# Two transformer blocks on one core: weights stored in load order, and the second attention by pairs of heads

## What is computed

```python
# block 1: attention, short convolution, then a mixture of experts
for g in range(N_GROUPS):                     # 4 groups of 8 experts, D_EXPERT = 256
    act = silu(einsum('nd,edf->nef', h, w_gate[sl])) * einsum('nd,edf->nef', h, w_up[sl])
    act = act * combine[:, g, :, None]        # 2 experts of 32 for each token
    y = y + einsum('nef,efd->nd', act, w_down[sl])
# block 2: grouped attention with 8 heads of 64 on 2 key heads, 512 + 256 keys
s = einsum('bqkgd,btkd->bkgqt', qblk, k) * scale
p = softmax(s.astype(float32), axis=-1)
o = einsum('bkgqt,btkd->bqkgd', p, v)
# beside it a long convolution, gates, and at the end a layer of
# 16384 small experts with 16 picks for each of 8 heads of a token
```

## Time and profile before

| | |
|---|---|
| median of 3 runs | 2894.65 us (2886.13 to 2894.65) |
| the profiled execution's own time | 2893.39 us |
| its span | 2891.6 us |
| mean granted PE clock, share of full | 0.957 |
| busy: PE, DVE, ACT, POOL | 2607.6, 1564.7, 1055.6, 516.1 us |
| DMA | 294127 packets, 605.99 MB |

### The profile page before, as it was taken

The page is one execution under the profiler, slowest core; times in us unless marked ns, Lnnn a source line. Parts: engine busy times, 40 slices in busy tenths (PEclk is TensorE's granted clock), DMA queues, the critical chain, the costliest instruction groups (busy, mean ns, idle before and its releaser), DMA issues.

```text
span 2891.6 us, 31507 instructions
## 1 busy us (share of the span) xinstructions
PE 2607.6 (90%) x12520; PEld 1910.5 (66%) x12520; DVE 1564.7 (54%) x2920; ACT 1055.6 (37%) x1317; POOL 516.1 (18%) x427
## 2 busy tenths in 40 slices
PE   6998997667778899999989999988888999999997
PEld 4666685422234344655768999988888877777775
DVE  4533244321126656454542998899998444444444
ACT  5754432120004311565233333444554333333332
POOL 0100000000010000000000011133334255555550
PEclk9999998788887999999999999999999999999998
DMA  5543442899980000201122466778999898989992
GB/s 184 196 146 117 174 146 89 279 375 371 376 323 30 29 29 29 88 30 40 48 89 88 157 228 230 257 265 319 349 350 345 292 315 312 323 312 323 312 325 90
DMA packets 294127, 605.99 MB, mean 210 GB/s; under 512 B 16503, under 2 KB 157943, under 8 KB 283800
## 3 DMA queue, kind: packets, MB, share of 16 engines
q1 hardware_dynamic: 223072, 384.33, 38.5%
q0 software_dynamic: 44528, 154.69, 14.9%
q10 hardware_dynamic: 26376, 64.90, 5.9%
HBM read 533.08 MB, written 70.78 MB: 209 GB/s over the span
## 4 chain that ended last, share of the span: by engine, by line
PE 62%; DVE 17%; DMA 8%; ACT 5%; SPq 4%; issue 3%; ACTq 0%; DVEq 0%
PE P L2670 6%; PE P L2671 6%; PE P L2672 6%; DVE window L592 4%; SPq L2759 4%; DMA ug<-in_ur,sparse 4%; PE P L2550 3%; PE P L2551 3%; PE P L2552 3%; PE P L2390 3%; DVE part L592 2%; PE P L2215 2%; PE P L2621 2%; PE P L2018 2%; DVE ug L1381 2%
## 5 line engine op out<-in xcount | busy, mean ns | idle before, releaser
L592 DVE TENSOR_TENSOR part<-raw,part 128x2048 fp32r<-128x2048 f32 x136 | 311.1, 2288 | 411.1 <-ACT part L1868 411.1
L2550 PE MATMUL P<-hr,part 128*128 128x384 f32 (+1 forms) x1136 | 400.1, 352 | 39.7 <-DVE part L592 39.2
L2551 PE MATMUL P<-hr,part 128*128 128x384 f32 (+1 forms) x1136 | 393.3, 346 | 0.0
L2552 PE MATMUL P<-hr,part 128*128 128x384 f32 (+1 forms) x1136 | 392.9, 346 | 0.0
L2685 POOL DMA_INDIRECT ug<-in_ur,sparse x128 | 163.9, 1281 | 1191.9 <-DVE window L600 816.6
L1868 ACT ACTIVATE part<-raw 128x2048 fp32r<-128x2048 f32 x136 | 260.8, 1917 | 289.0 <-PE P L2672 268.8
L2670 PE MATMUL P<-part,ge 128*128 128x512 f32 x768 | 302.9, 394 | 0.7 <-issue 0.7
L2671 PE MATMUL P<-part,ge 128*128 128x512 f32 x768 | 299.4, 390 | 0.0
L2672 PE MATMUL P<-part,ge 128*128 128x512 f32 x768 | 299.0, 389 | 0.0
L2550 PEld LDWEIGHTS P<-hr,part 128*128 128x128 f32 x1136 | 215.9, 190 | 50.9 <-DVE part L592 44.9
L2551 PEld LDWEIGHTS P<-hr,part 128*128 128x128 f32 x1136 | 216.1, 190 | 5.1
(11 more groups left out here) (369 smaller groups left out, 4568.3 us busy)
## 6 DMA issues: line engine op xcount, KB each, us to landing
raw<-in_u SPq DMA_DIRECT2D x64, 1024.0 KB, 5.1
raw<-in_v SPq DMA_DIRECT2D x64, 1024.0 KB, 6.3
W<-in_w_in SPq DMA_DIRECT2D x18, 2048.0 KB, 9.1
W<-in_ada_w SPq DMA_DIRECT2D x12, 2048.0 KB, 8.3
W<-in_w_gate SPq DMA_DIRECT2D x24, 1024.0 KB, 14.4
W<-in_w_up SPq DMA_DIRECT2D x24, 1024.0 KB, 16.6
a_scratch<-gt ACTq DMA_DIRECT2D x128, 192.0 KB, 3.7
w_scratch<-window ACTq DMA_DIRECT2D x12, 2048.0 KB, 11.1
```

Of the source, the lines that this page charges most:

```text
L592: return v.tensor_tensor(out=out_, in0=in0, in1=in1, op=op)
L2550: t.matmul(b, wh[:, k, js], HR[0][:, k, lo:S], start=k == 0, stop=False)
L2551: t.matmul(b, wh[:, k, js], HR[1][:, k, lo:S], start=False, stop=False)
L2552: ins = t.matmul(b, wl[:, k, js], HR[0][:, k, lo:S], start=False, stop=k == 7)
```

## The change

**Weights.** The host now stores every large weight so that a load's 4096 floats (2048 for the down weights of one expert, wq, u and v) stand in a row for each partition: `blocks` cuts a matrix into pieces of n columns and puts the rows of a partition beside each other, `rows` does so for a whole matrix. Gate and up of an expert become one array `w_up`, with 256 columns of gate and 256 of up beside each other for each k, as the slot has them; each expert is one transfer instead of two, with runs of 16 KB, and a pair's down weights one with runs of 8 KB. x, ctx, w_in, w_sb, w_conv, w_out, ada_w, w_in_2, w_attn, w_hy, w_out_2 and wq are stored so too. v has a second copy `vd` for the dense product (runs of 8 KB); gathers still read `v`. What a slot holds is the same as before. In the loop for further experts, which this input doesn't enter, the count of transfers goes from three to two.

**The second attention** runs over 16 iterations, a pair of heads (2j, 2j + 1) and 128 queries, with two heads' work in each. `PR` is one buffer for each head of the pair, and the scores have banks 0 to 3 for one iteration: neither is used by turns any more. `PT` holds 12 tiles of 128 queries, and is written and read in each iteration. Transposes come in three groups of four, into banks 4, 5 and 6, of which ACT copies the first and DVE the others. The sums of the iteration before are 12 matmuls of 128 columns (`pair_sums`), the two heads by turns into the two halves of the partitions of bank 6. A whole gate projection (`gate`, 24 matmuls) stands in an iteration.

```diff
-        PT = reg(4, 6).rearrange("p (k n) -> p k n", k=6)
+        PT = reg(4, 3).rearrange("p (k n) -> p k n", k=12)
...
-                slots.take(("up", e), 2)
-            slots.take(("down", i), 2)
+                slots.take(("up", e))
+            slots.take(("down", i))
...
-        for it in range(32):
-            AT_GATE[it] = [("w", it // 2 + 1)] * (it >= 2 and it % 2 == 0) + [("br", 1, it // 2 - 2)] * (it in (5, 7, 9, 11))
+        for it in range(16):
+            AT_GATE[it] = [("w", it + 1)] * (it >= 1) + [("br", 1, it - 2)] * (2 <= it < 6)
...
+            for it in range(17):
+                st = lambda i, h=slice(0, 2), c=16 * (it % 2): STT[:, c + 2 * i:c + 2 * i + 2][:, h]
+                one = lambda i, g_: st(i, slice(g_, g_ + 1))
+                n = 10 * it
+                if it < 16:
                     dve.wait_ge(s["s2_mm"], 2 * it + 1)
+                    dve.wait_ge(s["e2_a"], 4 * (it - 1))
+                    for g_ in range(2):
+                        v.tensor_reduce(out=one(0, g_), in_=bank[g_], axis=AX.X, op=MAX).then_inc(s["a2_v"], 1)
                     dve.wait_ge(s["s2_mm"], 2 * it + 2)
+                    for g_ in range(2):
+                        v.tensor_reduce(out=one(1, g_), in_=bank[2 + g_][:, 0:256], axis=AX.X, op=MAX).then_inc(s["a2_v"], 1)
+                    dve.wait_ge(s["a2_v"], n + 4)
                     tt(st(2), st(0), st(1), MAX).then_inc(s["a2_v"], 1)
+                    dve.wait_ge(s["a2_v"], n + 5)
                     ts(st(3), st(2), -0.125, None, MUL).then_inc(s["a2_v"], 1)
+                if it:
+                    dve.wait_ge(s["pv_mm"], it - 1)
+                    for x in (1, 2):
+                        dve.wait_ge(s["tr_mm"], 3 * (it - 1) + x + 1)
+                        v.tensor_copy(PT[:, 4 * x:4 * x + 4, :], k4(bank[4 + x])).then_inc(s["tr_v"], 1)
+                if it < 16:
+                    dve.wait_ge(s["e2_a"], 4 * it + 4)
                     tt(st(6), st(4), st(5), ADD).then_inc(s["a2_v"], 1)
+                    dve.wait_ge(s["a2_v"], n + 7)
                     v.reciprocal(st(7), st(6)).then_inc(s["a2_v"], 1)
+                    dve.wait_ge(s["a2_v"], n + 8)
+                    for g_ in range(2):
+                        ts(PR[g_], PR[g_], one(7, g_), None, MUL).then_inc(s["a2_v"], 1)
...
+            def result(n):
+                j, q = n // 4, n % 4
+                act.wait_ge(s["pv_mm"], n + 1)
+                a.activation(A2[:, j, q * 128:q * 128 + 128], bank[6][:, 0:128], ACT.Copy).then_inc(s["pv_a"], 1)
...
                 if it:
+                    act.wait_ge(s["pv_mm"], it - 1)
+                    act.wait_ge(s["tr_mm"], 3 * (it - 1) + 1)
+                    a.activation(PT[:, 0:4, :], k4(bank[4]), ACT.Copy).then_inc(s["tr_a"], 1)
+                if it < 16:
+                    st = lambda i, g_, c=16 * (it % 2): STT[:, c + 2 * i + g_:c + 2 * i + g_ + 1]
+                    act.wait_ge(s["a2_v"], 10 * it + 6)
+                    act.wait_ge(s["tr_mm"], 3 * it)
+                    for g_ in range(2):
+                        a.activation(PR[g_][:, 0:512], bank[g_], ACT.Exp, bias=st(3, g_), scale=0.125, accum_out=st(4, g_)).then_inc(s["e2_a"], 1)
+                    for g_ in range(2):
+                        a.activation(PR[g_][:, 512:768], bank[2 + g_][:, 0:256], ACT.Exp, bias=st(3, g_), scale=0.125, accum_out=st(5, g_)).then_inc(s["e2_a"], 1)
+                if it < 16:
                     for x in AT_GATE[it]:
                         high_piece(x)
+                    gate(it)
+                if it:
+                    result(it - 1)
...
+            def pair_scores(it):
+                j, q = it // 4, it % 4
+                pe.wait_ge(s["e2_a"], 4 * it)
+                for lo, hi, b in ((0, 512, 0), (512, 768, 2)):
+                    for g_ in range(2):
+                        ps = slice(64 * g_, 64 * g_ + 64)
+                        ins = t.matmul(bank[b + g_][:, 0:hi - lo], QQ[ps, j, q * 128:q * 128 + 128], KK[ps, lo:hi], start=True, stop=True)
+                    ins.then_inc(s["s2_mm"], 1)
+            def turn_pair(n):
+                pe.wait_ge(s["tr_a"], n)
+                pe.wait_ge(s["tr_v"], 2 * n)
+                for x in range(3):
+                    pe.wait_ge(s["a2_v"], 10 * n + (10 if x else 9))
+                    if x == 2:
+                        pe.wait_ge(s["pv_a"], n)
+                    for i in range(4):
+                        g_, k = (4 * x + i) // 6, (4 * x + i) % 6
+                        ins = t.transpose(bank[4 + x][:, i * 128:i * 128 + 128], PR[g_][:, k * 128:k * 128 + 128], ident)
+                    ins.then_inc(s["tr_mm"], 1)
+            def pair_sums(n):
+                b = bank[6][:, 0:128]
+                pe.wait_ge(s["tr_a"], n + 1)
+                pe.wait_ge(s["tr_v"], 2 * n + 2)
                 for i in range(6):
+                    for g_ in range(2):
+                        ps = slice(64 * g_, 64 * g_ + 64)
+                        ins = t.matmul(b[ps, :], VV[:, i, ps], PT[:, 6 * g_ + i, :], start=i == 0, stop=i == 5)
                 ins.then_inc(s["pv_mm"], 1)
 
+            for it in range(17):
+                if it < 16:
+                    pair_scores(it)
                 if it:
+                    turn_pair(it - 1)
+                if it < 16:
+                    gate(it)
+                if it:
+                    pair_sums(it - 1)
...
+            def whole(src, n=4096):
+                return [(0, n, lambda ap: ap, src)]
...
-                    load(key, [(0, 4096, lambda ap, lo=lo: k8(ap)[:, :, lo:lo + 256], A[name][key[1]].rearrange("(k p) n -> p k n", p=128))
-                               for lo, name in ((0, "w_gate"), (256, "w_up"))])
+                    load(key, whole(A["w_up"][key[1]]))
                 elif key[0] == "down":
-                    load(key, [(2048 * j, 2048 * j + 2048, k2, A["w_down"][2 * key[1] + j].rearrange("(k p) n -> p k n", p=128)) for j in range(2)])
+                    load(key, [(0, 4096, lambda ap: ap.rearrange("p (t n) -> p t n", t=2), A["w_down"][2 * key[1]:2 * key[1] + 2].rearrange("t p n -> p t n"))])
...
-                    load(key, cols(w2, 512 * key[1]))
+                    load(key, whole(w2[key[1]]))
...
+                    src = A["vd"][2 * c + half]
...
+    def blocks(w, n):
+        rows, width = w.shape
+        return w.reshape(rows // 128, 128, width // n, n).transpose(2, 1, 0, 3).reshape(width // n, 128, rows // 128 * n)
+    def rows(w):
+        return blocks(w, w.shape[1])[0]
...
+        "w_up": gate_up.transpose(0, 2, 1, 3).reshape(32, 128, 4096),
+        "w_down": I["w_down_e"][0].reshape(32, 2, 128, D).transpose(0, 2, 1, 3).reshape(32, 128, 2048),
```

More of the change, by code:

```diff
@@ L1169, in vector_program @@
             dve.wait_ge(s["iv_mm"], 8)
-            for it in range(33):
-                if it < 32:
-                    st = lambda i, c=8 * (it % 2): STT[:, c + i:c + i + 1]
-                    ba, bb, Pb, n = bank[it % 2], bank[2 + it % 2], PR[it % 2], 7 * it
+            for it in range(17):
[3 more added lines that the diff above has]
+                if it < 16:
@@ L1645, in layers @@
                     act.wait_ge(s["op_mm"], 8)
-                    a.dma_start(CX, A["ctx"].rearrange("(k p) n -> p k n", p=128)).then_inc(s["cx"], 16)
+                    a.dma_start(CX, A["ctx"].rearrange("p (k n) -> p k n", k=8)).then_inc(s["cx"], 16)
                     a.dma_start(ZF[0:33, :], A["zf"]).then_inc(s["lay"], 16)
@@ new lines, in gate @@
+            def gate(c):
+                act.wait_ge(s["gt_mm"], c + 1)
+                act.wait_ge(s["iv_mm"], 8)
+                act.wait_ge(s["iv_v"], 8)
+                a.activation((GA2 if c < 8 else GB2)[:, c % 8, :], bank[7], ACT.Sigmoid).then_inc(s["gt_a"], 1)
+            def result(n):
+                j, q = n // 4, n % 4
+                act.wait_ge(s["pv_mm"], n + 1)
+                a.activation(A2[:, j, q * 128:q * 128 + 128], bank[6][:, 0:128], ACT.Copy).then_inc(s["pv_a"], 1)
@@ L2460, in tensor_program, with gate @@
                 inverse_columns(c)
-            def gate_half(n):
-                c = n // 2
+            def gate(c):
                 key, raw, wh, wl = piece_of(c)
-                if n % 2 == 0:
-                    pe.wait_ge(s["ph_v"], max(HV2["w", c], HV2["h", 7]))
-                    pe.wait_ge(s["gt_a"], c)
-                for k in range(4 * (n % 2), 4 * (n % 2) + 4):
+                pe.wait_ge(s["ph_v"], max(HV2["w", c], HV2["h", 7]))
+                pe.wait_ge(s["gt_a"], c)
+                for k in range(8):
                     t.matmul(bank[7], wh[:, k, :], HH[:, k, :], start=k == 0, stop=False)
@@ L2483, in head_sums @@
+            def pair_sums(n):
+                b = bank[6][:, 0:128]
+                pe.wait_ge(s["tr_a"], n + 1)
+                pe.wait_ge(s["tr_v"], 2 * n + 2)
                 for i in range(6):
```

(39 more changed lines are left out.)

105 lines of the change are left out of this document (25 added, 80 removed).

## The result

The changed kernel takes **2803.73 us** (median of 4 runs, 2800.24 to 2810.21), the one before 2890.91 us beside it (4 runs); the ratio is 0.970, 95% interval 0.968 to 0.973. 2818 us was forecast, 2801 to 2854 as the range. Later the same kernel was run again, beside others: 2808.41 us (5 runs), ratio 0.971 [0.969, 0.973]. The profiled execution took 2804.89 us, its span is 2803.1.

A forecast was written before the change was run, and what follows sets the result against it. Bounds: transfers in the experts, PE in the second attention. Gains of 29 us (expert loads), 2 (other loads) and 44 (attention) sum to 75, taken from 2893.4 us: 2818 us, range 2801 to 2854.

The forecast's parts named there:

- Expert loads: Mixture of experts: 16 KB rows lift gate and up loads from 349 to 420 GB/s, gain 29 us (24 to 32).
- (b): Expert loop: loads are bound behind the queues at 370 GB/s and gain nothing; 2847 us, 5 in 100.
- Slots are no bound: Expert loop: six 2 MB slots suffice, with 20 us of loads still to come and slots free after 7 us.
- Other loads: Two 2 MB loads with 2 KB rows on the chain gain 1 us each, 2 us together.
- Attention: Second attention: rounds fall from 13.44 to 10.6 us (bounds 10.0 and 13.1), gain 45 us, net 44.
- The sums: Attention round: 24 instructions in couples of columns take 1.8 us, between 1.28 together and 2.82 one after the other.
- The gate: Attention round: a whole gate projection takes 5.80 us.
- margins: Attention's end: 3 us off for bare copies and exponentials, 2 us for uncounted changes of array shape.
- (a): Attention: row halves do not overlap (2842 us), or sums run one after the other (2834), both 2858; 13 in 100.
- (c): Whole change: no couples and no faster rows, only 5 us gained, 2888 us; 3 in 100.
- (d): Attention: single banks make the chain through ACT and DVE the bound, rounds 19.5 us, 2958 us; 3 in 100.
- if the time after 1480 us moves: Sign of being wrong: the sparse layer's length should not change; no size given.

The follow-up runs named there:

- the three lengths: Changed kernel with gate and up weights in runs of 1 KB, 2 KB or 4 KB instead of 16 KB; medians 2831.7, 2824.2 and 2811.7 us.
- heads_serial: Changed kernel with one head's score and sum products issued before the other's, and TensorE waiting between heads so they cannot overlap; 2855.05 us.
- after_again: The changed kernel run once more without any edit, as a base beside later kernels; 2808.41 us, ratio 0.971.
- runs_1k: Changed kernel with gate and up weights in runs of 1 KB instead of 16 KB, still one transfer per expert; median 2831.7 us.

## Why the prediction was right, and which terms were not

**Expert loads, 29 us: right.** From the gather of h_rows to the last second product the loop shrank from 833.00 - 527.20 = 305.8 to 802.13 - 527.61 = 274.5 us, 31.3, near the upper bound of 32; the slices lie at 410 to 437 GB/s where 420 was taken. The rule of the Trainium skill ("DMA: Bandwidth & Descriptors", section "Where 436 GB/s comes from") of some 358 GB/s for a core's HBM is not borne out by this program on one core: the mean was 413. With it rival (b) is out. What was overlooked is the cost to others: the write of h_rows, 6.2 us before, lands in 10.0, the gather of y_rows in 11.6 instead of 9.1, and with both on the chain the stage gave 28.0 us. That the runs set the rate was argued from two rows; the three lengths have shown it. "Slots are no bound" was too simple: SP's waits from 540 to 800 us are now 132.3 us for gate and up products and 108.4 for down products to free a slot, where from 546 to 822 us it had waited 20.8 and 12.7. With the DMA share at 1.00 in the loop no run shows that this costs anything.

**Other loads, 2 us: 1.1.** The two on the chain take 7.37 and 7.79 us after 7.96 and 8.32.

**Attention, 44 us: the mechanism right, the size 58.2.** The round was forecast as 10.6 and is 10.00, the lower bound. That it meets the bound is chance: the bound had 1.28 us for the sums and 5.80 for the gate. The sums were given 1.8 us and take 1.46, 5.4 us over the rounds: the surcharge for a second load of weights was not there, since one head's twelve alone take 1.47 too. By the Trainium skill's rule ("TensorE: Matmul & The Clock Gate", section "The mechanism" of part 3) the sums should have cost 2.8; they do cost 2.99, 0.2 of it the wait, when the halves are kept from working together, and 1.46 when not, so here couples of columns, each with its own load of weights, overlap in full. The gate was given 5.80, twice a half gate, and takes 5.59: each half had carried 0.1 us beside its products, 3.4 us over the rounds. The rest of the 14 us are margins: I took off 3 us for copies that lie bare and 2 for changes of shape. Bare are the 1.3 us of line 1190 and the 0.3 of line 1833. Before, the stage was 16 x 13.44 + 5.0 us, now it is 16 x 10.00 + 1.8, so the ends gave 3.1 us where the forecast had them cost 1.

**Rivals.** (a) is refuted by heads_serial: without overlap the whole takes 2855 us, near the 2858 of (a). (c) and (d) by the profile: the chain through ACT and DVE is ready some 3 us early.

**The sum.** 75 forecast, 88.5 by the profiles: 14 from the attention, 4.7 of clock that came by chance, less 3.6 of the same kind, and 1.9 less from the loads (28.0 + 1.3 - 0.2 where 31 was forecast). The 3.6 us would be a sign of being wrong by the prediction ("if the time after 1480 us moves"), but that stage took from 739.2 to 748.5 us in kernels that do not differ there, and 740.8 and 747.9 in two with the old layout. In after_again's execution the clock fell the other way (2811.81 us), and the gap to the forecast is half as large.

**The range.** Its lower end does not follow from its terms. With 431 GB/s and rounds of 10.0 the gain is 32 + 2 + 55 - 1 = 88 us and the time 2805; 2801 comes out only if the 5 us of margins are dropped too, which the prediction does not say. The first median, 2803.73, lies between the two, so that it fell inside the range is partly luck; the second, 2808.41, lies inside either.

## What to carry to other kernels

Ask for the packets' sizes wherever the queues are full: there each packet cost 7.5 ns of an engine on top of its bytes, so the layout that the host writes was worth 28 us, and moving two stray megabytes out of such a stretch some 4.4 us more. Two products on different halves of the array, rows or columns, cost here what one costs, but the program should set them alternately. And where the chain shows a load ahead of a product that does not read it, look at who gives back the bank: an order of four instructions was worth 8 us in its stage and some 6 in the whole.

## What the hardware showed that was not expected

- TensorE lets products of one half pass waiting ones of the other, three instructions in both places where it was seen: with four instructions ahead the overlap was whole (scores 1.50 us), with twelve only some 0.4 of 1.5 us (sums 2.38 against 2.8).
- Couples overlap at 128 columns too: 24 instructions with as many loads of weights in 1.46 us, 61 ns each, where one head's twelve alone took 1.47.
- Small transfers take longer beside the new loads: h_rows 10.0 us instead of 6.2 (median of four). With runs of 1 KB for gate and up it was 8.6 (runs_1k), so the length of their runs is the smaller part; what the rest is was not settled.
- The granted clock after the same wait is 1.00 in one execution of a kernel and 0.56 in the next, worth 4.6 us here.
